# Attention of an mLSTM layer: blocks that both directions read are multiplied once, and the heads are written out

## What is computed

```
def odd_mixer(h_ctx, h_lat, w_in, w_out, conv_w, conv_b, wq, wk, wv, w_if, b_if, norm_g, skip):
    def pre(h):
        xm, zg = jnp.split(h @ w_in, [ML_WIDTH], axis=-1)
        xcv = jax.nn.silu(centred_dwconv(xm, conv_w, conv_b))
        ...
        return xcv, zg, heads(headwise(xcv, wq)), heads(headwise(xcv, wk)), heads(headwise(xm, wv))
    ...
    hm_c, hm_l = prefix_bidir(mlstm_scan, (q_c, k_c, v_c), (q_l, k_l, v_l), ...)
    def post(hm, xcv, zg):
        hn = head_norm(hm, norm_g).astype(xcv.dtype)
        return ((hn + skip * xcv) * jax.nn.silu(zg)) @ w_out
```

```
h(t) = N0(t)/D0(t) + N1(t)/D1(t)
Nd(t) = sum over sources s of  p_d(t, s) v(s)      p_d = (q(t) . k(s)) * decay_d(t, s)
Dd(t) = max(|sum over s of p_d(t, s)|, exp(-m_d(t)))
```

## Time and profile before

| | |
|---|---|
| three runs | 2697.48, 2691.78, 2696.11 us |
| median | 2696.11 us |
| profiled execution: time / span | 2691.36 / 2689.7 us |
| TensorE clock granted, mean | 0.983 of full speed |
| PE busy | 2550.7 us, 95% of the span, 13319 instructions |
| PE's weight loads (PEld) | 1979.7 us, 74%, beside PE |
| DVE busy | 1530.1 us, 57%, 2359 instructions |
| ACT busy | 827.5 us, 31%, 994 instructions |
| POOL busy | 988.3 us, 37%, 1162 instructions |

### The profile page before, as it was taken

How to read it: one execution, slowest core, us unless ns; L and a number is a source line. 1 busy time by engine, 2 the same in 40 slices (tenths; PEclk the granted TensorE clock), 3 DMA queues, 4 the chain that set the end, 5 groups by cost and what they waited for, 6 DMA issues and landing times.

```text
span 2689.7 us, 37273 instructions
## 1 busy us (share of the span) xinstructions
PE 2550.7 (95%) x13319; PEld 1979.7 (74%) x13319; DVE 1530.1 (57%) x2359; ACT 827.5 (31%) x994; POOL 988.3 (37%) x1162
## 2 busy tenths in 40 slices
PE   7898899999999998999999999998999999999998
PEld 3787854545455667888877887777989889898787
DVE  3677765887875225524246664966465555646510
ACT  2425635263552113312122112123233241422210
POOL 0139967887800100211224433445334333331000
PEclk9999999999999999999989999999999999999999
DMA  7413320111106785351132333564131321215421
GB/s 295 121 57 92 97 76 27 48 32 43 51 16 215 252 266 157 100 183 36 36 98 95 124 117 125 177 230 153 44 116 54 106 88 63 100 35 173 133 94 47
DMA packets 272083, 293.95 MB, mean 109 GB/s; under 512 B 35232, under 2 KB 234184, under 8 KB 271568
## 3 DMA queue, kind: packets, MB, share of 16 engines
q1 hardware_dynamic: 202672, 209.75, 24.3%
q10 hardware_dynamic: 64672, 65.70, 7.4%
q0 software_dynamic: 4608, 16.78, 1.9%
HBM read 200.99 MB, written 91.20 MB: 109 GB/s over the span
## 4 chain that ended last, share of the span: by engine, by line
PE 69%; DVE 9%; issue 3%; ACT 3%; DMA 2%; POOL 1%; ACTq 0%; SPq 0%; DVEq 0%; POOLq 0%
PE ps L136 61%; PE ps L1372 6%; DVE xc_part L2536 1%; PE ps L1023 1%; ACT arena L1570 1%; DVE arena L2464 1%; ACT L1570 1%; DMA ml_z<-arena 0%; PE ps L1377 0%; DVE arena L528 0%; PE ps L1305 0%; DMA qk_map_full<-ml_qk_maps 0%; DVE arena L2453 0%; PE ps L1203 0%; DVE arena L2465 0%
## 5 line engine op out<-in xcount | busy, mean ns | idle before, releaser
L136 PE MATMUL ps<-h_full,weights 128*128 128x512 f32 (+1 forms) x1152 | 417.8, 523 | 8.7 <-ACT arena L1570 4.0
L136 PE MATMUL ps<-h_part,in_weight_parts 128*128 128x512 f32 (+1 forms) x1920 | 412.8, 376 | 13.7 <-POOL in_weight_parts L2879 6.5
L136 PEld LDWEIGHTS ps<-h_part,in_weight_parts 128*128 128x128 f32 x1920 | 337.0, 190 | 84.6 <-issue 8.1
L136 PEld LDWEIGHTS ps<-h_full,weights 128*128 128x128 f32 x1152 | 218.3, 190 | 201.5 <-issue 187.0
L136 PE MATMUL ps<-v_part,p_part 128*128 128x512 f32 x1248 | 296.7, 396 | 0.1
L136 PEld LDWEIGHTS ps<-v_part,p_part 128*128 128x128 f32 x1248 | 235.4, 191 | 49.6 <-issue 0.8
L136 PE MATMUL ps<-q_part,xc_part 128*128 128x256 f32 x1920 | 244.4, 286 | 3.9 <-DVE q_part L2569 3.9
L136 PEld LDWEIGHTS ps<-q_part,xc_part 128*128 128x128 f32 x1920 | 234.1, 192 | 4.9 <-DVE q_part L2569 4.5
L136 PE MATMUL ps<-arena,weights 64*16 64x128 f32 (+2 forms) x896 | 177.3, 388 | 16.0 <-ACT arena L1570 14.4
L1372 PE MATMUL ps<-wo_part,mx_part 128*128 128x512 f32 x768 | 183.9, 400 | 5.2 <-DVE mx_part L2536 4.8
L2873 POOL TENSOR_TENSOR in_weight_parts<-weights,ones 128x1024 fp32r<-128x1024 f32 x32 | 81.3, 2541 | 258.3 <-PE ps L136 188.0
(11 more groups left out here) (396 smaller groups left out, 4119.1 us busy)
## 6 DMA issues: line engine op xcount, KB each, us to landing
weights<-in_e_w_in SPq DMA_DIRECT2D x32, 512.0 KB, 5.1
weights<-in_o_w_in SPq DMA_DIRECT2D x32, 512.0 KB, 4.5
arena<-in_mod_w POOLq DMA_DIRECT2D x24, 512.0 KB, 5.6
ml_xcv<-arena ACTq DMA_DIRECT2D x16, 640.0 KB, 2.9
xc_full<-ml_xcv SPq DMA_DIRECT2D x4, 2560.0 KB, 10.5
xm_tiles<-ml_xm SPq DMA_DIRECT2D x15, 640.0 KB, 3.8
arena<-in_mod_w SPq DMA_DIRECT2D x4, 2048.0 KB, 21.3
s_out_maps<-arena ACTq DMA_DIRECT2D x32, 256.0 KB, 3.3
```

Source lines behind the costliest of these rows:

```text
L136: return nc.tensor.matmul(o, lhsT, rhs, start=(k == 0), stop=(k == n - 1))
```

## The change

1. *Shared sources once.* For a source block that a quarter's queries read in both directions, h has p0 v/D0 + p1 v/D1 = (p1 + p0 D1/D0) v/D1 (or the same the other way round). These are the two context blocks, and for each query block its own block on the diagonal. The changed kernel multiplies such a piece once: `row_step` makes the row D1/D0 for all queries and adds the scaled piece to its partner. A quarter then has 20 pieces of 128 by 128 instead of 26. Each other piece goes on as before. For the row:
   - `row_sums` on PE multiplies a 128 x 128 matrix of ones with `Sp`, so that both sums over sources stand in every partition of a PSUM bank (a new slot, "d"; the slots of a head are 44 instead of 40);
   - the rows of exp(-m) come from a new DRAM tensor (`em_d`, written once by ACT) with two DMAs of SP per quarter (`em_rows_in`) into `em_rows`;
   - `row_step(q, n)` on DVE, n = 0 to 3: max and negated max over 512 columns, both reading PSUM; reciprocal and product of 256; product and sum of 512 for the context pair; product and sum of 256 for the diagonal pair.
2. *Order.* `weighted` first multiplies the pieces that are not shared, then the shared ones (`value_sums`, `shared_sums`). High and low parts of the shared pairs are made after the row steps (`shared_high`, `shared_low`; `SPLITS` is their order). On DVE `head_out` is cut into `denominators`, `numerators` and `normed`, and the sum of `mixed` becomes `added`, later in the queue. Two value splits of the next head stand ahead of the output of quarter 3.
3. *Heads.* The loop over heads 1 and 2 is written out on all five engines.
4. *Ahead of head 0.* On SP the loads of the skip rows go (the first two stay, the others are issued by ACT after its stores of a gate tile), the columns and decay rows come at tile 14, and DVE takes the queries of quarter 1 before the skip product of the last gate tile.
5. *Layer 0.* `batch_rows` of the last scan batch stands behind the first part of `y_full`, not the second.
6. *Tail.* The last head's two transposes stand at output weights 6 and 9 instead of 4 and 7, and the splits of the first output weights around `head_out` are reordered.

The core of the diff (left out: the same on engines that mirror it, and layouts):

```diff
         for p in range(NPR):
-            SLOTS += [("v", p + 6), ("s", 1, p)]
-        SLOTS += [("v", 11), ("q", 3, 0), ("q", 3, 1)] + [("s", q, p) for q in (2, 3) for p in range(NPR)]
+            SLOTS += [("v", p + 6), ("s", 1, p)] + [("d", 0)] * (p == 1)
+        SLOTS += [("v", 11), ("q", 3, 0), ("q", 3, 1)]
+        for q in (2, 3):
+            for p in range(NPR):
+                SLOTS += [("s", q, p)] + [("d", q - 1)] * (p == 0)
+        SLOTS += [("d", 3)]
...
-        def sources(q, j, d):
+        def shared_pair(q, p):
+            return p == 0 or 2 * p == CBLK + 2 * q
...
+        def sources(q, j):
+            J0 = CBLK + 2 * q
+            J = J0 + j
+            early = [(I, 0) for I in range(CBLK, J0)] + [(I, 1) for I in range(J0 + 2, NBLK)]
+            late = [(J0, 0) if j else (J0 + 1, 1)] + [(J, 0), (0, 0), (1, 0)]
+            return early, late
...
-                if q == 1:
+                if q == 0:
                     sp.wait_ge(*past("f_mm0", NB // 2 - 1))
                     batch_rows(NB - 1, 0, "f_in3")
...
+            def em_rows_in(i, q):
+                if not (isinstance(i, int) and i == 0 and q < 2):
+                    sp.wait_ge(*past("ps_ready", 8 * i + (2 * q - 2)))
+                for d in range(2):
+                    o = QW * (1 - d)
+                    sp.dma_start(EB[:, q % 2, o:o + QW], em_row(i + MH * d, q)).then_inc(sem(f"em_in{q % 2}"), 16)
...
             for m in range(MT):
                 input_weight((MT + m) // 2, m % 2)
-                if m >= 2:
-                    skip_rows(m - 2)
-                if m == 13:
+                if m == 1:
+                    for x in range(2):
+                        skip_rows(x)
+                if m == 14:
                     sp.wait_ge(*past("rows_t", 1))
-                    sp.wait_ge(*past("xr_stored", 32))
+                    sp.wait_ge(*past("xr_stored", 64))
                     column_rows_in(0)
                     decay_rows(0)
...
+            def row_sums(i, q):
+                pe.wait_ge(*past("sums", 36 * i + (9 * q + 9)))
+                mm(slot(i, "d", q), ones[:, :], Sp[:, q % 2], 0, 1).then_inc(sem("lo_mm"), 1)
...
             def weighted(i, q):
                 for j in range(2):
                     value_sums(i, q, j)
+                if q == 2:
+                    row_sums(i, 3)
+                for j in range(2):
+                    shared_sums(i, q, j)
                     weight_sums(i, q, j)
...
             head(0, False)
-            with pe.Fori(1, MH - 1) as i:
+            for i in range(1, MH - 1):
                 head(i, False)
             head(MH - 1, True)
...
+                def row_step(q, n):
+                    z = q % 2
+                    E = EB[:, z]
+                    r0, r1 = E[:, QW:2 * QW], E[:, 0:QW]
+                    if n == 0:
+                        dve.wait_ge(*past(f"em_in{z}", 64 * i + (32 * (q // 2) + 32)))
+                        dve.wait_ge(*past("lo_mm", slot_done(i, "d", q)))
+                        den = slot_bank("d", q)
+                        rlink(V.tensor_tensor(E, den, E, ALU.max))
+                        V.scalar_tensor_tensor(out=E, in0=den, scalar=-1.0, in1=E, op0=ALU.mult, op1=ALU.max).then_inc(sem("vq_ev"), 1)
+                        dve.wait_ge(*past("vq_ev", NEV * i + EVICTED["d", q]))
+                    elif n == 1:
+                        rlink(V.reciprocal(r1, r1))
+                        rlink(V.tensor_tensor(r0, r0, r1, ALU.mult))
+                    elif n == 2:
+                        a, b = PAIR_AT[q][0]
+                        x = PR[:, z, a:b].rearrange("p (i d c) -> p i d c", i=2, d=2)
+                        rlink(V.tensor_tensor(x[:, :, 0], x[:, :, 0], r0.unsqueeze(1).to_broadcast([P, 2, QW]), ALU.mult))
+                        V.tensor_tensor(x[:, :, 1], x[:, :, 1], x[:, :, 0], ALU.add).then_inc(sem("ps_ready"), 1)
...
                 for p in range(NPR):
                     value_low(p + 6)
                     weigh(1, p)
+                    if 1 <= p < 4:
+                        row_step(0, p - 1)
                 value_low(11)
+                weights_low(1, NPR - 1)
+                row_step(0, 3)
                 for h in range(2):
                     query_low(i, 3, h)
-                weights_low(1, NPR - 1)
+                shared_low(0)
                 for q in (0, 1):
                     head_out(q, 0)
                     head_out(q, 1)
                     for p in range(NPR):
                         weigh(q + 2, p)
+                        for n in ((0, 1), (2,), (3,), (), ())[p]:
+                            row_step(q + 1, n)
                         if p in (2, 4):
                             mixed(i, q, p // 2 - 1)
-                    weights_low(q + 2, NPR - 1)
+                        if p == 4:
+                            added(i, q)
+                        if p == 3:
+                            shared_low(q + 1)
...
+                for n in range(2):
+                    row_step(3, n)
                 head_out(2, 0)
                 if not last_head:
                     maps_low(i + 1)
-                    columns_low(i + 1)
+                    columns_low(i + 1, (0,))
                 head_out(2, 1)
+                for n in (2, 3):
+                    row_step(3, n)
                 if not last_head:
-                    first_queries(i + 1, (lambda: mixed(i, 2, 0), lambda: mixed(i, 2, 1)))
+                    columns_low(i + 1, (1, 2, 3))
+                shared_low(3)
+                normed(2)
+                if not last_head:
+                    first_queries(i + 1, (lambda: mixed(i, 2, 0), lambda: mixed(i, 2, 1), lambda: denominators(3, 0), lambda: added(i, 2)))
+                    value_low(0, i + 1)
+                    value_low(1, i + 1)
+                    numerators(3, 0)
+                    head_out(3, 1)
+                    normed(3)
```

301 lines of the change are left out of this document (215 added, 86 removed).

## The result

The changed kernel takes 2674.33 us, the median of 5 runs (2670.57 to 2679.72), against 2696.11 us before: a ratio of 0.9926, 95% interval 0.9909 to 0.9943. That is 20 to 22 us or 0.7% faster, where 41 us (2655) was forecast. The profiled execution took 2673.97 us; its span is 2672.3 us against 2689.7, so 17.4 us less, where the working gave 37.6.

The account below looks back on a forecast made before the run. TensorE matmuls were taken to bound middles, DVE's chain with ACT the seams; -22.6 + 3.4 - 3.9 - 3.2 + 1 - 9 - 3.3 = -37.6 from 2691.4 gave 2653.8, stated as 2655 us. Range 2643 to 2666, wider 2626 to 2676.

Parts of the forecast that it names:

- No wait: Score stretches of quarters 2 and 3: PE would not wait, though DVE ends 6 us behind and catches up under the sums.
- the price of the row steps: Eight added DVE operations per quarter, priced from the nearest rows of the earlier trace: 5.8 us.
- The matmuls: Attention: 960 matmuls instead of 1248, -66 us, plus 14 us of row sums; net -52 us if PE waited no longer.
- Seams: Quarter 2 sums to the next head's fourth value tile: 53.6 us each, -3.2 us over three.
- DVE's chain, longer by 5.8 us, takes their place: Seams: the 8 us of matmuls leaving each would not come off, because DVE's longer chain replaces them.
- Middles: Fourth value tile to quarter 2's sums: -22.6 us of matmuls, +3.4 of new waits, -3.9 of a wait that goes.
- the three waits in quarter 1: Quarter 1 of each head: two score slots and the last value tile late by 0.4, 0.15, 0.3; +3.4 us over four heads.
- B: Rival: DVE's row steps and POOL's operations exclude each other in SBUF, giving 2673 us; chance 14%.
- Before the attention: Up to head 0: weight and first scores earlier, less a PE wait of some 4 us two value tiles later; -9 us.
- The even layer: `s_lags` DMAs go ahead of the second part of `y_full`, shortening PE's wait of 5.99 us; -3.3 us.
- Tail: Last head's quarter 2 sums through the output weights: 86 us instead of 84.8, +1 us; matmuls removed leave as waits.
- The loop: Second seam: 2.07 us in which DVE begins the loop body again without waiting would go with the loop.

Follow-up runs that it names:

- e7: Changed kernel with all operands of the DVE row steps 2 columns wide, shared weights not combined rightly: 2656.79 us, 0.9854 of the kernel before.
- e4: Changed kernel with the next head's first scores weighed and third value tile split ahead of the second half of quarter 3's output: 2660.95 us, ratio 0.9871.
- e6: Kernel before the change with only the loop over heads 1 and 2 written out: 2692.81 us, ratio 0.9991.
- e11: Changed kernel with the parts outside the attention undone (`batch_rows`, SP's loads, quarter 1 queries, transpose places): 2671.74 us, ratio 0.9911.
- e13: Changed kernel with the parts outside the attention undone and the loop over heads 1 and 2 kept: 2680.25 us, ratio 0.9947.
- e1: Changed kernel with SP's two skip-row loads behind the weight of gate tile 2 instead of tile 1: 2669.21 us, ratio 0.9904.
- e2: Changed kernel with the last head's two transposes back at output weights 4 and 7: 2666.42 us, ratio 0.9893.
- e5: Changed kernel with heads 1 and 2 as a loop again on all five engines: 2682.76 us, ratio 0.9950.

## Why the prediction was wrong

The direction and the kind of effect were right, the size was half: 20.2 us of the working's 37.6 failed. By terms of its sum: 9.3 us in the middles, where "No wait" and the price of the row steps failed; 6.8 ahead of gate tile 11, 6.0 of them a wait on SP's queue that the working put at nothing; 4.6 in the tail; 2.8 ahead of head 0; and the seams came out 3.3 us better than forecast. By its own steps:

- **The matmuls**: right. The four sums of a quarter take 14.6 us (2045.84 to 2060.41) where they took 18.7, and 960 matmuls are left. A row sum adds 0.85 us (9.57 from 2060.41 to 2069.98, 8.72 at the same place before), forecast 0.88.
- **Seams**: right that most of the matmul time does not come off, and where. The walk gave 53.6 us each, with PE waiting 5 us at the fourth value tile on `p_full`; measured 52.9, 53.2, 51.4 with 4.0, so -6.5 us in all for a forecast of -3.2. But "DVE's chain, longer by 5.8 us, takes their place" is half of it: without the work of the row steps (e7) a seam is 3.2 us shorter, some 1 us of that by the clock, and the 4.0 us remain. They belong to a line on DVE that the matmuls had covered before; e4 shows that it could have been cut.
- **Middles**: -23.1 forecast, -13.8 measured; 9.3 us, the largest miss. Two things cost more: 1.6 us behind each seam at the lower clock (4.9 us; the wait was foreseen, what follows a wait was not), and in the score stretches "No wait" failed: the second transpose waits 0.6 us for `mixed`, with what follows 0.75, eight times 6.0 us. One thing cost less: the three waits in quarter 1, forecast at +3.4, came to 0.4 us a head, 1.6. The sum took the row steps at the durations of the earlier trace rows, without POOL beside them; they are 1.4 us longer there. The text had the earlier trace rows before it, took 0.3 us for one split of four, and made the collision a rival (B, 14%) instead of a term. Its 5 us for waits at the score slots were close to the 6.0 measured; its 14 us for three seams did not come, since in the seams POOL is idle beside these steps.
- **Before the attention**: -9 forecast, -6.2 measured. The first scores came 13.7 us earlier, forecast 12.9 (1854.48 - 1789.52 = 65.0 us behind the small transposes before, 51.3 now); the wait behind them was 5.3 us, not 4, and again the lower clock behind it took 2.8 (the value tile and its 24 matmuls take 6.14 us from start to start, 3.32 at full speed). The kernel before has a loss of this kind there too, 0.6 us on the scores at 1854.48 (3.76 for 3.12), and its stretch is 72.0 us in this trace but 73.6 to 74.5 in e6, e11 and e13, which have its order: part of the 2.8 us that are missing may be scatter.
- **The wait on SP that was not seen** (+6.0 us): the working read SP's queue at gate tiles 12 to 15, where it had a question, and not at tile 1, where the change had put two loads, the first with waits of its own, ahead of the weight of tile 2. The order stood in the diff (`if m == 1`), and the prediction says "no wait on `in_weight_parts`". This is the step that failed by omission, e1 shows it.
- **The even layer**: the wait for `s_lags` fell from 5.99 to 2.85 us, -3.15 of a forecast -3.3. But little of it reaches layer 1. From the small transposes ahead of that wait (1008.38 and 1008.14 us) to the first product of layer 1 it is 389.6 us before and 388.5 in the changed kernel; in the kept traces with the new order 388.2 to 390.6, with the old one 389.6 to 389.9 and once 393.8. What comes back lies between the first output product and layer 1: 375.4 us in three traces with the old order, 377.5 to 378.4 in the thirteen with the new one, but 377.9 in e11 too, which has the old one. The cause, and how much of the term is left, stay open: no run has this edit alone.
- **Tail**: +1 forecast, +5.6 measured. "Its last two `mixed` come two weights later" was walked on DVE alone. Behind the last `mixed` stand the splits of weights 10 to 15, so that the later transpose holds back PE's own next operands; e2 gets 9.6 us out of it. With that the tail is 4.1 us shorter than before, so that "matmuls that leave here leave as waits" holds for the order that was chosen, not for the change.
- **The loop**: in the forecast it was worth the 2.07 us of the earlier trace rows. It is worth 8.0 in the changed kernel (e5).

The result lies 8.3 us above the main range (2643 to 2666). The wider one (2626 to 2676) holds it at its edge because it takes B in, and this is in part luck: B's mechanism gave some 6 us of the miss, and the rest is the lower clock, SP's queue and the place of the transposes, which neither range had priced.

## What to carry to other kernels

Where a walk through the queues finds a wait of some microseconds on TensorE, add what the matmuls behind it lose at the lower clock; both go together when the wait goes. Of a step that is moved, walk the queue at its new place as well as at its old one, to the next instruction that somebody waits for: here a load with a wait ahead of a weight, and a transpose whose consumer stands ahead of the next splits, each took back 6 to 10 us. Durations for work that is added on DVE are to be taken from rows where the engine beside it does what it will do there.

## What was not expected of the hardware

- Three waits of 0.9, 0.7 and 0.7 us in a row brought TensorE's clock to its lower level in some seams and not in others of the same program: 12 matmuls in 4.61 or 3.03 us.
- 20 useless matmuls (4.6 us of work) in the place of a wait of 4.0 us cost 0.2 to 0.6 us there and gave back 1.6 us behind it, at each of three places.
- A DVE operation of 256 columns with two inputs from SBUF takes 0.84 to 0.97 us beside POOL's additions and 0.42 alone. L2788, with the same kind of operands, is not touched: it had begun before POOL's addition, and there it is POOL that waits (1.12 us instead of 0.74).
- The jump of a loop cost 2.8 us by the medians in one order of the work (0.9981 to 1.0000 is its interval) and 8.0 in another.
